# Seven norms cut into token halves, and layer 2's modulation pairs at other blocks, in a three-layer transformer kernel

## The reference, cut to what matters

```python
h = modulate(rms_norm(x, norm1_g[l]), sh1, sc1)
hc = modulate(rms_norm(xc, norm1_g[l]), csh1, csc1)
... # in projection, attention, pool and conv (layers 0, 1) or MLA and HGRN2 (layer 2)
x = x + g1 * jnp.einsum('blm,md->bld', mix, w_out[l])
x = x + g2 * swiglu(modulate(rms_norm(x, norm2_g[l]), sh2, sc2), w_ffn_in[l], w_ffn_out[l])
... # the same for xc in layer 0 alone
return rmsnorm(x, g_final)
```

## Time and profile before

| | us |
|---|---|
| median of 3 runs | 2543.85 |
| lowest and highest | 2540.05, 2545.73 |
| the profiled execution | 2540.79 |
| its span, first to last instruction | 2539.0 |

### The profile page before, as it was taken

The page is one execution under the profiler, slowest core; times in us unless marked ns, Lnnn a source line. Parts: engine busy times, 40 slices in busy tenths (PEclk is TensorE's granted clock), DMA queues, the critical chain, the costliest instruction groups (busy, mean ns, idle before and its releaser), DMA issues.

```text
span 2539.0 us, 30987 instructions
## 1 busy us (share of the span) xinstructions
PE 2424.5 (95%) x13121; PEld 2025.8 (80%) x13121; DVE 1321.0 (52%) x1693; ACT 801.1 (32%) x1101; POOL 883.2 (35%) x633
## 2 busy tenths in 40 slices
PE   7999899999999999899999999998999989999998
PEld 4889778788888888688777778877998677888886
DVE  2898674655443443795656655655563443111113
ACT  2233662311111112425732122224443453222222
POOL 2006002233333342365034445543453003444442
PEclk9898899999999999999999999998999999999999
DMA  8232103224434242232034546531213102242331
GB/s 268 90 113 90 47 15 117 83 84 133 125 102 123 85 131 84 66 109 76 1 100 134 153 143 180 154 116 50 68 34 100 34 1 67 71 112 83 91 100 59
DMA packets 309227, 240.60 MB, mean 95 GB/s; under 512 B 10692, under 2 KB 304831, under 8 KB 309087
## 3 DMA queue, kind: packets, MB, share of 16 engines
...
...
## 4 chain that ended last, share of the span: by engine, by line
PE 87%; DVE 8%; ACT 3%; issue 1%; POOL 0%; DMA 0%; DVEq 0%; SPq 0%; ACTq 0%
PE ps L2592 63%; PE ps L1265 5%; PE ps L2627 3%; PE ps L1028 2%; DVE mod_w L2226 1%; PE ps L1285 1%; PE ps L682 1%; DVE mod_ctx L2226 1%; PE ps L765 1%; PE ps L990 1%; PE ps L738 1%; PE ps L2507 1%; PE ps L2544 1%; DVE small L1153 1%; DVE xg L2203 1%
## 5 line engine op out<-in xcount | busy, mean ns | idle before, releaser
L1735 POOL TENSOR_TENSOR w_lo<-raw,w_hi 128x512 fp32r<-128x512 f32 x518 | 757.2, 1491 | 1349.6 <-ACT w_hi L1843 1349.5
L2592 PE MATMUL ps<-h_hi,w_hi 128*128 128x512 f32 x1994 | 647.4, 371 | 25.3 <-DVE h_lo L2190 22.0
L2592 PE MATMUL ps<-h_lo,w_hi 128*128 128x512 f32 x1994 | 637.9, 366 | 0.0
L2592 PE MATMUL ps<-h_hi,w_lo 128*128 128x512 f32 x1994 | 637.3, 365 | 0.0
L1843 ACT ACTIVATE w_hi<-raw 128x2048 fp32r<-128x2048 f32 (+2 forms) x155 | 265.0, 1709 | 573.3 <-PE ps L2592 369.5
L2592 PEld LDWEIGHTS ps<-h_hi,w_hi 128*128 128x128 f32 x1994 | 339.0, 190 | 93.9 <-issue 23.2
L2592 PEld LDWEIGHTS ps<-h_hi,w_lo 128*128 128x128 f32 x1994 | 338.6, 189 | 66.2
L2592 PEld LDWEIGHTS ps<-h_lo,w_hi 128*128 128x128 f32 x1994 | 339.1, 190 | 65.2 <-issue 0.2
L2117 ACT ACTIVATE xg<-ps 128x512 f32<-128x512 f32 (+1 forms) x66 | 44.3, 671 | 678.2 <-PE ps L2592 491.6
L2226 DVE SCALAR_TENSOR_TENSOR mod_w<-mod_w,cond 128x512 f32<-128x512 f32 x217 | 234.5, 1080 | 3.4
L2592 PE MATMUL ps<-hid_hi,w_hi 128*128 128x512 f32 x704 | 232.0, 370 | 0.0
...
## 6 DMA issues: line engine op xcount, KB each, us to landing
...
```

The lines of the kernel that those rows point to most:

```text
L1735: ins = pool.tensor_tensor(w_lo[:, s, at:end], raw[:, s, at:end], w_hi[:, s, at:end].bitcast(F32), ALU.subtract)
L2592: ins = pe.matmul(ps[0:m, at:at + tw], weight(part, k, cols), v[:, held[k] if held else k, t0:t0 + tw], start=(at_k == 0 and j == 0 and no ...
```

## The change

- **Halves.** Norms 1, 2, 3, 5 and 6 are made in two halves of the tokens: 512 and 256 columns where the context runs along (1, 2), 256 and 256 else. The last two blocks of the stage before (late_blocks) and, for norms 1, 3 and 5, the first two of the next one (first_blocks) are cut the same way: first half of both tiles of block 2, of block 3, then the second halves, with the sums (norm_sums) and the turn (norm_turn) of the first half between second-half tiles; then the next stage's first block for the first half, with the second half's sums and turn in it. VectorE adds all seven squares to n_acc, so there are no sums on sq.
- **Norm 4** takes the context half at blocks base_ffn[1] + 30 to 32 and the latent half at the end. Layer 2's first products begin with the context's.
- **Norm 0.** Its sums stand after the third modulation product and its turn after the sixth; gscale is made in parts with the mods.
- **The end.** The output's transposes of the first half of the tokens stand between the second half's sums and turn.
- **Weights.** Whole blocks go to early_hi and early_lo (2048 columns): blocks n0 + 3 and n0 + 6 around each split norm, n0 being the first of the stage's last four. Blocks n0 + 4 and n0 + 5 use the other slot. Block n0 + 5 is rounded by ScalarE in four pieces between the first half's tiles.
- **Groups** are 6, 5, 5, 6; the pairs of layers 1 and 2 lie at other blocks, and the 16-step pairs of layer 2 are spread over three blocks instead of two. In layer 1 two rotations on VectorE come after the conv's mean instead of before it.

```diff
...
-GROUPS = (6, 6, 6, 4)
+GROUPS = (6, 5, 5, 6)
...
-        place([(2, p) for p in range(12)], [base_ffn[1] + 1 + 3 * p for p in range(12)])
+        place([(2, p) for p in range(12)], [base_ffn[1] + b for b in (2, 5, 9, 12, 15, 19, 21, 23, 26, 28, 30, 33)])
...
+        late_first = {1: base_out[0], 2: base_in[1] - 4, 3: base_out[1], 5: base_out[2], 6: blocks_used - 4}
+        early_blocks = [base_in[2] + 1] + [n + 3 for n in late_first.values()] + [
+            n + 6 for ni, n in late_first.items() if ni < 6]
+        swapped_blocks = [n + d for ni, n in late_first.items() if ni < 6 for d in (4, 5)]
+        def slot(n):
+            return 1 - n % 2 if n in swapped_blocks else n % 2
...
+        HALVES = {1: [(0, LAT), (LAT, CTX)], 2: [(0, LAT), (LAT, CTX)], 4: [(LAT, CTX), (0, LAT)]}
+        SPLIT = (1, 2, 3, 5, 6)
+        def halves_of(ni):
+            return HALVES.get(ni, [(0, LAT // 2), (LAT // 2, LAT // 2)])
...
+        LATE = {(2, 0, 0): 1, (2, 0, 1): 2, (3, 0, 0): 3, (3, 0, 1): 4, (2, 1, 0): 5, (3, 1, 0): 6}
...
+        CTX_BLOCK = base_ffn[1] + 30
...
             n = base_in[2]
-            block_ready(n, n % 2, n // 2)
-            products(n, KD, 256, spans(TOK), h_hi, h_lo, lambda k: pe.wait_ge(n_h, KD * 4 + k + 1), None, None,
-                     lambda s, t, t0: 1024 + CTX * t if t0 else 512 * t)
+            wh, wl = views(n % 2, KD, 256)
+            block_ready(n, 0, n // 2)
+            pe.wait_ge(n_h[0], KD * 4 + KD)
+            first_products(wh, wl, 0, 1024, LAT, CTX)
+            norm_sums(4, 1)
+            first_products(wh, wl, 1, 1024 + CTX, LAT, CTX)
+            pe.wait_ge(psum_free[1], (n + 1) // 2)
+            norm_turn(4, 1)
+            pe.wait_ge(lo_ready, n + 2)
+            for t in range(2):
+                ins = first_products(*early_views(n + 1, 256), t, CTX_FIRST_AT + CTX * t, LAT, CTX)
+            ins.then_inc(in_tile, 1)
+            first_products(wh, wl, None, 0, 0, LAT, lambda k: pe.wait_ge(n_h[1], KD * 3 + k + 1)).then_inc(gemm_done, 1)
...
+                next_hi(n0)
+                squares_of_block(ni, n0, 0)
+                split_hi(n0 + 3)
+                squares_of_block(ni, n0, 1)
+                act.wait_ge(gemm_done, n0 + 2)
+                if n0 + 4 < blocks_used:
+                    split_hi(n0 + 4)
+                for t in range(2):
+                    act.wait_ge(late_added, late_base(ni) + LATE[2, 0, t])
+                    norm_square(ni, 0, 4 + t)
+                warm_root(ni, 0)
+                for t in range(2):
+                    act.wait_ge(late_added, late_base(ni) + LATE[3, 0, t])
+                    norm_square(ni, 0, 6 + t)
...
+                def piece_of_next(i):
+                    if n0 + 5 < blocks_used:
+                        act.wait_ge(gemm_done, n0 + 3)
+                        each = block_floats(n0 + 5) // 4
+                        split_hi(n0 + 5, each * i, each * (i + 1))
...
+                third, each = n0 + 6, block_floats(n0 + 6) // 4
+                if ni == 2:
+                    act.wait_ge(gemm_done, n0 + 4)
+                    split_hi(third)
+                norm_root(ni, 1)
+                for m in range(KD):
+                    norm_tile(ni, 1, m)
+                    if ni != 2 and m % 2 == 0:
+                        act.wait_ge(gemm_done, n0 + 4)
+                        split_hi(third, each * (m // 2), each * (m // 2 + 1))
...
+            def late_adds(ni, n0, l, chunk, gain, mods_needed, pair=None):
+                def add(b, h, t):
+                    n, (t0, tw) = n0 + b, halves_of(ni)[h]
+                    c, at, m = 1 if t0 == LAT else 0, half_at(n, t, h), 2 * b + t
+                    if (b, h, t) in LATE:
+                        dve.wait_ge(late_done, late_base(ni) + LATE[b, h, t])
+                    else:
+                        dve.wait_ge(gemm_done, n0 + b + 1)
+                    xt = x[:, m, t0:t0 + tw]
+                    dve.scalar_tensor_tensor(xt, ps[:, at:at + tw], modc[:, l % 2, chunk + m, c:c + 1], xt, ALU.mult, ALU.add
+                                             ).then_inc(late_added if (b, h, t) in LATE else psum_free[n % 2], 1)
+                add(2, 0, 0)
+                add(2, 0, 1)
+                norm_add(ni, 0, 4)
+                add(3, 0, 0)
+                norm_add(ni, 0, 5)
+                add(3, 0, 1)
+                norm_add(ni, 0, 6)
+                norm_add(ni, 0, 7)
+                if pair:
+                    dve.wait_ge(late_pair, 1)
+                    pair_out(dve.tensor_copy, pair, pair_columns(n0 + 2))
+                if ni < 6:
+                    norm_gain(ni, gain, mods_needed)
+                norm_spread(ni, 0)
...
+                        for b, t in LATE_ADDS[ni][m]:
+                            add(b, 1, t)
+                        for i in LATE_SUMS[ni][m]:
+                            norm_add(ni, 1, i)
...
+                norm_tiles(ni, 0, {m: after(m) for m in range(KD)})
...
+                norm_spread(ni, 1)
+                norm_tiles(ni, 1)
...
+            def pair_share(m, ahead):
+                if m[0] == 2 and pair_both(m):
+                    return ((11, 16), (5, 11), (0, 5))[ahead]
+                steps = 2 * KD if pair_both(m) else KD
+                return ((steps // 2, steps), (0, steps // 2), (0, 0))[ahead]
...
+                        if n == CTX_BLOCK:
+                            for k in range(1, KD):
+                                norm_add(4, 0, k)
+                        if n == CTX_BLOCK + 1:
+                            norm_gain(4, A_GM, pairs_saved((2, 3)))
+                            norm_spread(4, 0)
+                        if n == CTX_BLOCK + 2:
+                            norm_tiles(4, 0)
...
+                    if i == 3:
+                        norm_sums(0, 0)
+                    if i == 6:
+                        norm_turn(0, 0)
...
+            def norm_sums(ni, h):
+                first, end = half_range(ni, h)
+                pe.wait_ge(n_added[h], NORM_ADDED * (ni - h + 1))
+                token_columns(pe, sums_at(ni, h), n_acc[:, first:end], (end - first) // P, True, True).then_inc(n_ss[h], 1)
+            def norm_turn(ni, h):
+                first, end = (v // P for v in half_range(ni, h))
+                pe.wait_ge(n_spread[h], ni - h + 1)
+                for j in range(end - first):
+                    at = rstd_at(ni, h) + P * j
+                    ins = pe.transpose(ps[:, at:at + P], wide(ni)[:, j, :], ident)
+                ins.then_inc(n_turned[h], 1)
...
+            def late_blocks(ni, n0, k_tiles, hi, lo, order=None, held=None, pair=None):
+                two, three = n0 + 2, n0 + 3
+                sp_ = halves_of(ni)
+                def part(n, h, t):
+                    done = late_done if (n - n0, h, t) in LATE else gemm_done
+                    half_tile(n, k_tiles, hi, lo, t, h, sp_[h], order, held).then_inc(done, 1)
+                block_ready(two, 0, freed(two))
+                part(two, 0, 0)
+                part(two, 0, 1)
+                block_ready(three, 1, freed(three))
+                part(three, 0, 0)
+                part(three, 0, 1)
+                if pair:
+                    pair_sum(pair, pair_columns(two)).then_inc(late_pair, 1)
+                part(two, 1, 0)
+                norm_sums(ni, 0)
+                if pair:
+                    pe.wait_ge(mod_saved, pairs_saved(pair))
+                part(two, 1, 1)
+                norm_turn(ni, 0)
+                part(three, 1, 0)
+                part(three, 1, 1)
...
+            def first_blocks(ni, n):
+                sp_ = halves_of(ni)
+                def ready(h):
+                    return lambda k: pe.wait_ge(n_h[h], KD * (ni - h) + k + 1)
+                pe.wait_ge(lo_ready, n + 1)
+                pe.wait_ge(late_added, late_base(ni) + LATE[2, 0, 1])
+                half_tile(n, KD, h_hi, h_lo, None, 0, sp_[0], None, None, ready(0),
+                          {4: lambda: norm_sums(ni, 1), 7: lambda: norm_turn(ni, 1)})
+                pe.wait_ge(lo_ready, n + 2)
+                pe.wait_ge(late_added, late_base(ni) + LATE[3, 0, 1])
+                for t in range(2):
+                    half_tile(n + 1, KD, h_hi, h_lo, t, 0, sp_[0])
+                pe.wait_ge(psum_free[0], freed(n))
+                half_tile(n, KD, h_hi, h_lo, None, 1, sp_[1], None, None, ready(1)).then_inc(gemm_done, 1)
+                pe.wait_ge(psum_free[1], freed(n + 1))
+                for t in range(2):
+                    ins = half_tile(n + 1, KD, h_hi, h_lo, t, 1, sp_[1])
+                then = block_pair(n + 1)
+                if then:
+                    ins = then()
+                ins.then_inc(gemm_done, 1)
...
+            pe.wait_ge(n_xg[0], KD * 6 + KD)
+            turn_out(0)
+            turn_out(1)
+            norm_sums(6, 1)
+            turn_out(2)
+            turn_out(3)
+            norm_turn(6, 1)
```

(3 more changed lines are left out.)

640 lines of the change are left out of this document (386 added, 254 removed).

## The result

The changed kernel took **2497.38 us** (median of 4 runs, 2495.11 to 2499.71), the kernel before 2541.95 in the same job (2537.36 to 2545.73): ratio 0.9825, 95% interval 0.9804 to 0.9845, some 44 us faster. I had forecast 2479, a gain of 64.6; the profiled span fell from 2539.0 to 2495.7 us, by 43.3. The time lies inside the range, but a third of the gain that I summed is missing.

A forecast was written before the change was run, and what follows sets the result against it. TensorE's own work bounds the kernel, leaving its idle and low-clock time to win. Norms 0 to 5 55.2 + last norm 5.8 - half tiles 1.4 + pairs 5 = 64.6 us, from 2540.79 to 2476.2, about 2479 as median; range 2456 to 2502.

The forecast's parts named there:

- Rival (c): Half tiles everywhere: bound by weight loads at 190 ns, not by columns; 66 us lost, 2545, no change; chance 0.03.
- Rival (d): At every half VectorE becomes the bound, each GpSimd catch on the path, 16.6 us a norm; 2558, slower; chance 0.05.
- (a): At the split norms GpSimd and VectorE don't meet: 12.5 us less, 2466; chance 0.14.
- (b): Weights late: block n0+5 rounded only after block 2 is done, 5 us at each of five places, 2504; chance 0.06.
- From the second half on TensorE has a whole block's first half (5.7 or 11.2 us) as cover: At the split norms: argument against VectorE becoming the bound, since TensorE has products to run meanwhile.
- the walk of norm 1: Timeline of norm 1's halves: turn done at 31.6, last tile at 46.2, needed at 47 to 48; no wait.
- The pairs, +5: Layer 2's modulation pairs: of 9.8 us of mod_w waits and the low clock behind, 5 gained; ends -5 and +13.
- VectorE beside GpSimd, -12.5: Norms 1, 2, 3 and 5: GpSimd's rounding slows h_lo, 3.1 us of waiting each, 12.5 in all.
- the row: Profile row: two-SBUF-input VectorE instruction takes 1.78 us beside GpSimd, 0.74 after; taken as 1.04 us a catch.
- This gives back all 10.9 us of low clock: Windows of 13 us after the six norms: time lost to lower clock, 10.9 us together, counted as fully regained.
- Conv, rotation and attention keep their work: Conv, rotation and attention stages: work unchanged, no gain or loss entered in the sum.
- The last norm: After the last product: 20.7 us of norm and output become 14.9, gain 5.8, between 3 and 8.

The follow-up runs named there:

- The run with two shares: The changed kernel with the 16 VectorE steps of layer 2's first four pairs shared over two blocks (8 and 8) instead of three: 2503.93 us, ratio 0.9834.
- both edits: The changed kernel with norm 2's second-half turn among block 1's products and ScalarE's copies of block 0 ahead of the context tiles: 2486.60 us, ratio 0.9764.

## Why the prediction was right in direction and the gain 20 us too large

**What held.** TensorE's own work sets the time, and its idle and its slow time at the norms is what was won: by layer 1's first product 25.4 of the 27.5 us of my terms were there. (Norm 0 is not cut in halves, as the title might suggest: its sums and turn only stand earlier.) Norm 1 went as walked: from the turn to the eighth tile 14.6 us on paper; in the trace VectorE starts on them at 430.8 and ends at 447.7, 16.9 us, of which 3.0 are the catches. The sums on n_acc alone, the clock at the upper level through norms 1, 3, 4 and 5, the first product at 66.3 (65 forecast), the largest pair wait in block 33 (3.7): as written. Rival (c) falls: the half tiles of the last group step at 0.11 us with one weight load each, and not at the 0.19 that a load shows. These are TensorE's last ones:

```profile
2479.14 0.28 PE L2912 MATMUL ps<-hid_lo,early_hi 128*128 128x256 f32 x1
2479.26 0.28 PE L2912 MATMUL ps<-hid_hi,early_lo 128*128 128x256 f32 x1
2479.37 0.28 PE L2912 MATMUL ps<-hid_hi,early_hi 128*128 128x256 f32 x1
```

Rival (d) falls with the waits for h_lo, 3.1 us in all. Rivals (a) and (b) were each near: without the meeting 6 to 8 us are to be had, and with the pieces later 12 are lost.

**What failed.**

1. *"From the second half on TensorE has a whole block's first half (5.7 or 11.2 us) as cover"*, and the walk of norm 1 taken for all norms. At norm 2 the second half's turn does not stand behind a first block's first half but ahead of block 2 of the in-projection, and the eight context tiles share ScalarE with the copies that free the PSUM banks. I followed VectorE and GpSimd through each half and never ScalarE. Price: 10 us at once, and some of the conv's 2.2 behind it; moving the turn and the copies brought back 12.2.
2. *The pairs, +5.* Nothing of it came: 9.1 us of waits after, 9.8 before, and one of 1.4 on w_lo beside them that the kernel before does not have. The step that failed is that I let one wait stand (block 33) and took all others as gone. The three-block share won its 5 us or more; the two-block spacing at blocks 26 to 28 put a load on the path, and block 33 cost 5 with its clock.
3. *VectorE beside GpSimd, -12.5*, was too dear. I let each of four pieces catch an h_lo at 1.04 us, at four norms. At norm 1 four catches are 3.0 us together, two of them on n_acc adds, and the whole cause is worth 6 to 8. The Trainium skill (SBUF — State Buffer, "Who interferes with whom") has the one that issues second blocked while the other's instruction runs, which I priced at a full GpSimd piece, up to 1.86 us a catch; the four catches here cost 0.37 to 1.09, so the row was the better guide to the price. Without this error on the safe side the forecast would have been further off.
4. *"This gives back all 10.9 us of low clock"*, and *"Conv, rotation and attention keep their work."* They kept their work but not their time. Over the three attentions 2.4, 5.1 and 2.0 us are lost. The granted clock is at the lower level for 75 us in them, where the kernel before has 58; 17.3 us at half the clock are 8.6 of these 9.5. I had given low clock a price only behind a new wait at a norm.
5. *Smaller ones.* Norm 0 won 8.1 of 10.0: the modulation products behind its early sums ran slow. The last norm: from the last product to the end 21.0 us have become 16.1 (14.9 forecast).

By stage, from the starts in the table above (us gained; the forecast column is the prediction's terms, apart from rounding its 64.6):

| stage | forecast | measured |
|---|---|---|
| norm 0 | 10.0 | 8.1 |
| layer 0's attention | 0 | -2.4 |
| norms 1 and 2, to layer 1's first product | 17.5 | 19.7 |
| norm 2's second half, to block 3 | 0.3 | -10.0 |
| conv and attention of layer 1 | 0 | -7.0 |
| norm 3, to the first down block | 5.8 | 9.8 |
| pairs and norm 4 | 18.8 | 13.8 |
| layer 2's attention | 0 | -2.0 |
| norm 5 | 7.9 | 10.2 |
| half tiles; layer 2's feed-forward with the last norm's first-half sums and turn | -1.4 | -1.8 |
| the end | 5.8 | 4.9 |
| sum | 64.7 | 43.3 |

The surplus of 8.5 us at norms 1, 2, 3 and 5 is the error on the safe side of point 3 (some 5) and, at norm 3, 1.6 of a pair's wait that stood there before; the rest I can't place. That the time fell inside the range is partly luck: against losses of 10 us at norm 2, 9.5 in the attentions and 5 at the pairs stood a price that was some 5 us too high.

**What stays open.** The attention of layer 1 ran at the lower clock for 17 us in the changed kernel and 10 before. With the turn early it is 14 us, and 10 in the two runs that have the copies first as well; in the runs with the other edits it is 14 to 17. The run with two shares has 14 us, and 3 us more lost between conv and attention, though its edit lies behind both: part of this differs from execution to execution. No run isolates what brings the clock down there. The rest of the conv's lateness (2.7 us on conv_acc with both edits) wasn't tried further, nor were the 2.8 us on w_lo at block 3, which the kernel before has too (3.2).
